# Two-layer hybrid encoder trunk: the mixer's vector work in the order of its inputs, without filler products, and its output projection begun over the tiles that are ready

## The reference, cut to what matters

```python
for l in range(DEPTH):                      # DEPTH = 2
    shift, scale, gate = ada_modulation(c, w_ada[l, 0], b_ada[l, 0])
    h = rmsnorm(x, g_norm[l, 0]) * (1.0 + scale) + shift
    y = hybrid_mixer(h, positions, l, ...)
    x = x + gate * rmsnorm(y, g_norm[l, 1])
    ...
    y = swiglu(h, ...) if l % 2 == 0 else moe_swiglu(h, ...)
    x = x + gate * rmsnorm(y, g_norm[l, 3])

def hybrid_mixer(h, ...):
    (q1, q2, k1, k2, va, qb, kb, vb, ob, ib, fb, cq, ckv, kr) = jnp.split(h @ w_in, split_idx, axis=-1)
    out_a = diff_attention_group(q1, q2, k1, k2, va, ...)       # 4 heads: 8 softmax units
    out_b = mlstm_group(qb, kb, vb, ob, ib, fb, ...)            # convolution, gates, 6 heads
    out_c = mla_group(cq, ckv, kr, ...)                         # 6 heads, rotary part
    return jnp.concatenate([out_a, out_b, out_c], axis=-1) @ w_out
```

## Time and profile before

| | |
|---|---|
| median of 3 runs | 1777.48 us (1775.68 to 1781.73) |
| profiled execution, its own time | 1780.08 us |
| its span | 1778.3 us |
| PE, DVE, ACT, POOL busy | 1535.9, 711.9, 545.2, 63.3 us |
| mean granted TensorE clock | 0.936 of full speed |
| mean DMA rate | 275 GB/s |

### The profile page before, as it was taken

The page is one execution under the profiler, slowest core; times in us unless marked ns, Lnnn a source line. Parts: engine busy times, 40 slices in busy tenths (PEclk is TensorE's granted clock), DMA queues, the critical chain, the costliest instruction groups (busy, mean ns, idle before and its releaser), DMA issues.

```text
span 1778.3 us, 30628 instructions
## 1 busy us (share of the span) xinstructions
PE 1535.9 (86%) x12500; PEld 1230.3 (69%) x12501; DVE 711.9 (40%) x1022; ACT 545.2 (31%) x749; POOL 63.3 (4%) x66
## 2 busy tenths in 40 slices
PE   5998879999999988776566999979998659999894
PEld 3757759999977577564344886559987448888552
DVE  2153245555531622410003884136764035666212
ACT  2123133333321231210003673035562024554101
POOL 0010000000000100100000000000000000000002
PEclk8989989999999899988777999999999889999898
DMA  9714556545433234659999999997677996555694
GB/s 362 272 42 178 215 196 265 211 180 189 176 138 142 67 152 184 260 233 425 423 424 425 426 397 387 425 425 300 256 277 280 424 422 264 238 236 224 269 424 161
DMA packets 74562, 488.92 MB, mean 275 GB/s; under 512 B 9792, under 2 KB 13920, under 8 KB 16544
## 3 DMA queue, kind: packets, MB, share of 16 engines
q1 hardware_dynamic: 72176, 479.94, 67.1%
q10 hardware_dynamic: 1648, 4.59, 0.7%
q0 software_dynamic: 576, 2.10, 0.4%
HBM read 482.66 MB, written 3.93 MB: 274 GB/s over the span
## 4 chain that ended last, share of the span: by engine, by line
PE 75%; DMA 10%; DVE 5%; issue 4%; ACT 3%; POOL 1%; SPq 1%; ACTq 1%; POOLq 0%; DVEq 0%
PE PG L1289 8%; PE PG L1399 5%; PE PG L1333 5%; DMA ring<-in_experts 4%; PE Y L909 4%; PE TRB L1333 4%; DMA arena<-in_experts 4%; PE Y L1301 4%; PE Y L1361 4%; PE Y L1173 3%; PE Y L917 3%; PE PG L873 3%; PE PG L874 3%; PE PG L875 3%; PE TRB L1339 3%
## 5 line engine op out<-in xcount | busy, mean ns | idle before, releaser
L1289 PE MATMUL PG<-ring,mixT 128*32 128x128 f32 (+1 forms) x1920 | 116.9, 347 | 61.2 <-issue 61.2
L1482 ACT ACTIVATE parts<-ring 128x2048 fp32r<-128x2048 f32 x84 | 158.5, 1906 | 12.3 <-PE Y L875 8.2
L1289 PEld LDWEIGHTS PG<-ring,mixT 128*32 128x32 f32 (+1 forms) x1920 | 89.5, 138 | 91.9 <-issue 76.7
L2272 DVE COPY arena<-TRB 128x64 f32<-128x64 f32 (+1 forms) x70 | 17.6, 252 | 335.6 <-PE TRB L1275 335.6
L1482 ACT ACTIVATE rope<-PG 64x128 f32<-64x128 f32 (+2 forms) x84 | 27.2, 324 | 373.0 <-PE PG L1289 348.4
L873 PE MATMUL PG<-h_parts,parts 128*128 128x256 f32 x448 | 127.5, 285 | 10.2 <-DVE parts L2148 10.2
L1289 PE MATMUL PG<-arena,mixT 128*32 128x128 f32 (+1 forms) x1664 | 98.9, 343 | 42.0 <-issue 42.0
L874 PE MATMUL PG<-h_parts,parts 128*128 128x256 f32 x448 | 127.3, 284 | 0.0
L875 PE MATMUL PG<-h_parts,parts 128*128 128x256 f32 x448 | 127.1, 284 | 0.0
L1289 PEld LDWEIGHTS PG<-arena,mixT 128*32 128x32 f32 (+1 forms) x1664 | 76.1, 135 | 69.5 <-issue 56.3
L2148 DVE TENSOR_TENSOR parts<-ring,parts 128x2048 fp32r<-128x2048 f32 x42 | 95.9, 2292 | 25.6 <-ACT parts L1482 25.4
(11 more groups left out here) (362 smaller groups left out, 2781.9 us busy)
## 6 DMA issues: line engine op xcount, KB each, us to landing
ring<-in_experts SPq DMA_DIRECT2D x168, 1024.0 KB, 13.3
arena<-in_experts SPq DMA_DIRECT2D x168, 1024.0 KB, 16.1
ring<-in_weights SPq DMA_DIRECT2D x116, 1024.0 KB, 6.1
ring<-in_weights SPq DMA_DIRECT2D x4, 512.0 KB, 4.3
ypairs<-hT ACTq DMA_DIRECT2D x3, 512.0 KB, 6.6
tok<-in_x SPq DMA_DIRECT2D x1, 1024.0 KB, 8.9
result<-scr SPq DMA_DIRECT2D x2, 512.0 KB, 2.6
ring<-in_weights SPq DMA_DIRECT2D x2, 432.0 KB, 6.3
```

Of the source, the lines that this page charges most:

```text
L1289: last = mm(bank[i * n:(i + 1) * n, 0:width], xe[:, k, 0:n], w[k // 4][:, k % 4, i * width:(i + 1) * width], start=(k == 0), stop=(k == KD ...
L1482: return nc.scalar.activation(out_, in_, func, **kw)
```

## The change

Five things are changed in both mixers.

1. The gate chain of the mLSTM goes to the head of the softmax work on ScalarE and VectorE. The convolution is cut in three parts of 8 operations, `conv(0)` to `conv(2)`, each behind its inputs, and `combine` follows its exponentials. The row maxima and exponentials of the last four A units go in TensorE's order (4, 6, 5, 7).
2. TensorE takes `at(0)` behind the second pair of A units and `at(1)` behind the last ones; `ada_rows` stands between the second and the third rotation. The three `busy` calls of the mixer are gone.
3. `pt(0)`, `c_unit(4)`, `pt(1)`, `c_unit(5)` stand between the two halves of the value projection `vb`; VectorE copies the halves out (`values`) in two places.
4. `bo` moves from the TR ring to the PJ ring.
5. The transposes into `mixT` are regrouped: `mt0` (tiles 0, 1) ahead of the mLSTM scores, `mt1` and `mt2` (5, 6, 7) behind `bo`, `mt3` and `mt4` (2, 3, 4) when `tok_ready` is set. Column blocks 2 and 3 of the output projection are computed over tiles 0, 1, 5, 6, 7 first and over 2, 3, 4 later; then blocks 0 and 1 follow. The third `ada_rows` stands between. The weight order is 2, 3, 0, 1.

```diff
-        uses.extend(("out", l, c) for c in range(D // SW))
+        uses.extend(("out", l, c) for c in OUT_ORDER)
...
+OUT_ORDER = (2, 3, 0, 1)
+MIX_EARLY, MIX_LATE = (0, 1, 5, 6, 7), (2, 3, 4)
...
                 def at(h):
                     bank = take_tr((f"at{h}", l))
-                    if h >= 2:
-                        busy(bank, 4 if h == 2 else 2)
...
                 def pt(u):
-                    if u == 1:
-                        busy(bank, 4)
...
+                at(0)
                 fm_pair("qk1", keys[6])
                 for b in range(TB):
                     a_units((2, b), (3, b))
+                at(1)
                 fm_pair("qk2", keys[7])
...
+                turn(0)
+                turn(1)
                 ada_rows(ADA_MIXER[l][1])
-                at(0)
-                at(1)
+                turn(2)
+                turn(3)
...
+                for b in range(TB):
+                    pe.wait_ge(*tr_done(f"co{b}", l))
+                turn_mixed("mt1", 5, 6)
+                turn_mixed("mt2", 7)
...
+                for i in range(3):
+                    pe.wait_ge(*tr_done(f"mt{i}", l))
+                for b in range(2):
+                    sc_over(b)
+                    mixed(2 + b, MIX_EARLY)
+                ada_rows(ADA_MIXER[l][3])
+                pe.wait_ge(tok_ready, l + 1)
+                turn_mixed("mt3", 2, 3)
+                turn_mixed("mt4", 4)
+                ada_columns(ADA_MIXER[l][3])
+                pe.wait_ge(*tr_done("mt3", l))
+                pe.wait_ge(*tr_done("mt4", l))
+                for b in range(2):
+                    mixed(2 + b, MIX_LATE).then_inc(out_read, 1)
+                for b in range(2):
+                    sc_over(2 + b)
+                    pe.wait_ge(pj_free[b], len(PJ_LAYER) // 2 * (l + 1))
+                    mixed(b, MIX_EARLY)
+                    mixed(b, MIX_LATE).then_inc(y_full if b else out_read, 1)
...
                 ada_rows(ADA_MIXER[l][0])
+                ae.wait_ge(gate_in, l + 1)
+                run(g_e[0:BH, :], g_n[0:BH, :], ACT.Exp).then_inc(gate_exp, 1)
...
+                negmaxes("a", 0, 1)
+                conv(0)
                 combine(0)
...
+                values(0)
                 r = root(("a", l))[:, 0:8].rearrange("p (b h o) -> p b h o", b=TB, o=1).to_broadcast([P, TB, AH, AV])
```

More of the change, by code:

```diff
@@ L1052, in mixer, with turn @@
                 pe.wait_ge(*pj_done("uq2", l))
-                for i in range(4):
+                def turn(i):
                     bank = take_sc((("rot", i), l))
@@ L1103, in mixer, with turn_mixed @@
                 last.then_inc(tr_full, 1)
+                def turn_mixed(name, *tiles):
+                    bank = take_tr((name, l))
+                    for j, f in enumerate(tiles):
+                        for b in range(TB):
+                            last = nc.tensor.transpose(bank[:, j * T + b * P:j * T + (b + 1) * P],
+                                                       tok[:, b, f * P:(f + 1) * P], ident)
+                    last.then_inc(tr_full, 1)
+                pe.wait_ge(*tr_done("ao", l))
+                turn_mixed("mt0", 0, 1)
                 pe.wait_ge(qks_ready, l + 1)
@@ L1141, in mixer @@
                 for b in range(TB):
[L1142 removed]
+                    bank = take_pj((f"bo{b}", l))
                     for h in range(BH):
@@ L1147, in mixer @@
                             last = mm(o, scw[:, h, c:c + P], vbx[:, kb, h, :], start=(kb == 0), stop=(kb == b))
[L1148 to L1169, removed]
+                    last.then_inc(pj_full, 1)
+                for b in range(TB):
+                    pe.wait_ge(*tr_done(f"co{b}", l))
@@ L1170, in mixer, with mixed @@
+                turn_mixed("mt1", 5, 6)
+                turn_mixed("mt2", 7)
+                def mixed(c, tiles):
                     s = slot("out", c)
                     for j in range(2):
-                        for k in range(KD):
+                        for k in tiles:
                             last = mm(Yk[:, 2 * c + j, :], ring[:, s, k, j * P:(j + 1) * P], mixT[:, k, :],
-                                      start=(k == 0), stop=(k == KD - 1))
-                    last.then_inc(out_read if c < D // SW - 1 else y_full, 1)
+                                      start=(j == 0 and k == 0), stop=(k == MIX_LATE[-1]), skip_group_check=True)
+                    return last
@@ new lines, in sc_over @@
+                def sc_over(b):
+                    pe.wait_ge(sc_free[b], len([i for i in range(len(SC_LAYER) * (l + 1)) if i % 4 == b]))
+                for i in range(3):
[7 more added lines that the diff above has]
+                turn_mixed("mt4", 4)
@@ L1613, in mixer @@
                 run(em[:, :], bank[:, 12:24], ACT.Exp).then_inc(free, 1)
+                bank, free = tr_item("mt0")
+                run(mixT[:, 0:2, :], bank.rearrange("p (a t) -> p a t", a=2), ACT.Copy, scale=gd[:, l:l + 1]).then_inc(free, 1)
                 ae.wait_ge(*tr_done("gt", l))
@@ L2079, in mixer @@
                 ve.wait_ge(obt_ready, l + 1)
-                bank, free = tr_item("mt1", l)
+                bank, free = tr_item("mt3", l)
                 for j in range(2):
@@ L2084, in mixer @@
                 last.then_inc(free, 1)
-                bank, free = tr_item("mt2", l)
-                V.scalar_tensor_tensor(mixT[:, 4, :], bank[:, 0:T], gml[:, l, 2:3], obt[:, 2, :], ALU.mult, ALU.mult)
-                V.tensor_copy(mixT[:, 5, :], bank[:, T:2 * T]).then_inc(free, 1)
+                bank, free = tr_item("mt4", l)
+                V.scalar_tensor_tensor(mixT[:, 4, :], bank[:, 0:T], gml[:, l, 2:3], obt[:, 2, :], ALU.mult,
+                                       ALU.mult).then_inc(free, 1)
                 ada(ADA_MIXER[l][3])
```

123 lines of the change are left out of this document (63 added, 60 removed).

## The result

The changed kernel takes 1750.18 us (median of 4 runs, 1746.31 to 1754.32), the kernel before 1777.61 in the same session: ratio 0.9844, 95% interval 0.9824 to 0.9864. It is 27 us faster, where 44 were forecast; 1750 lies above the range of 1728 to 1747. The profiled execution took 1752.9 us.

What follows compares the result with a forecast made beforehand. TensorE, nearly without pause in both mixers, was taken as the bound: its products, few waits and half-clock work. Gains of 20.7 us (mixer 0) and 23.2 (mixer 1), together 43.9, gave 1733.6 us, range 1728 to 1747.

Steps and rivals of the forecast that it cites:

- Gate chain first: Ahead of the rotations: gate chain moved before the first row maxima, ending near 84; the 2.35 us pause goes.
- Clock around the rotations: Rotations and conditioning product run at full clock without the pause ahead: gains of 2.96 and 2.32 us a mixer.
- the split: Rotations divided into 1.7 and 1.3 us, both shorter than the 2.35 us rest before the fall, so full clock.
- Rival B: Clock falls again at rotations and conditioning product (1744) or among transposes with short waits (1743); both 1753; chance 0.22.
- The Trainium skill's rule: Transposes don't count as clock work like products; stretches of `pt` and `mt` transposes would be rest, sum up to 9 us smaller.
- Filler of `at` and `pt(1)`: In each mixer, filler and waits at `at` go, gain 3.2 us; waits and filler at `pt(1)` go, net 7.0.
- The wait for VectorE at `pt(1)`: New wait: VectorE takes `values(0)` before the product freeing the bank of `pt(1)`; TensorE waits about 0.4 us.
- Output projection: From `bo` to the projection: early products hide group B's chain, waits of 4.4 become 1.5, gain 2.9 us a mixer.
- rivals D and E: Transfers give TensorE's gain back, no effect, chance 0.03; or late tiles of `vb` stall the engines, slower, chance 0.03.

Runs made afterwards that it cites:

- the padded kernel: The whole change plus 66 TensorE instructions at the start (16 one-column products and three met waits), experts' code where it was before: 1734.58 us.
- -42 and -26: The changed kernel with 24 more instructions (met waits) and with 40 more (10 one-column products) at TensorE's start: 1743.53 us and 1745.30 us.
- the first part alone: Against the changed kernel: output projection in the order of before, 74 padding instructions at the start; vector order, rotations and removed filler kept: 1741.81 us.
- the second part alone: Against the kernel before: only the output projection over the ready tiles first; vector order, filler and rotations of before: 1771.53 us.
- the last pair of runs: The whole change with 74 instructions of met waits ahead of `x`, 1733.03 us, and with 75 in three places where TensorE is idle, 1733.58 us.

## Why the prediction was wrong

**The step that failed:** "The dense part in between is TensorE's own work and the experts' transfers start on `y_full`, so both move as a whole." The dense part did (303.5 and 303.6). The experts grew by 15.3 us. The sum had no term for what fewer instructions do to code that is reached by branches. The 16.6 us between forecast and result are these 15.3 and 2.0 of the start, less 0.7 that the mixers gave above the forecast. At the position of before the same change takes 1734.6, against the forecast 1733.6; that they are so close is in part luck, since in its trace the padded kernel is 1.7 us shorter up to mixer 0 and 2.6 in the dense part than before, and 3.3 longer in the rest. That the position is the cause is shown from both sides, by the change without it and by it without the change, and the first run followed it product by product (26, 14, 6, whole). That a wait for the next block of instructions is how the position acts is the reading that fits these counts and the packets; no row shows the wait itself. The wide experts lose only at the change's position, the narrow ones also at -42 and -26; which single pause belongs to which landing was not resolved, nor why the pause ahead of the last expert is 9.5 to 9.9 at those two. Why the rest of the padded change is up to 5 us longer than that of others at its position stays open.

**Gate chain first.** Right: it runs from 82.73 to about 86.0 on VectorE, where about 84 was forecast for its end, still ahead of the first row maxima (88.07), and the 2.35 us are gone.

**Clock around the rotations.** The gain came (1.90 and 1.47 for the rotations, where 1.7 and 1.3 were forecast, and 3.66 for the product). The reason given for it, the split, was wrong: together they run at full clock too. What the runs leave of the reason is the missing pause, which the prediction also named; that the number held although the split does nothing is in part luck. Rival B did not occur at either of its places. The Trainium skill's rule (TensorE: Matmul & The Clock Gate, Part 4, PE-mode transpose) did not cost anything in this change: the clock was 1.00 through the stretches of transposes of 0.8 to 1.3 us with waits of up to 0.9 about them. Whether the rule is right, no run here shows: where the clock fell among transposes, in mixer 1 before and with the first part alone, a wait of 2.37 us stood ahead of them.

**Filler of `at` and `pt(1)`.** Right in size: mixer 0 as a whole gained 21.0 with 20.7 forecast, mixer 1 23.6 with 23.2, and from the end of the first half of `vb` to the second `ada_rows` it is 10.3 us (149.62 to 159.94), where 10.7 was forecast. With its filler back a mixer gave up 4.2. The wait for VectorE at `pt(1)` was put at 0.4 and is 0.47. The convolution, cut in three, costs VectorE 0.9 us more, put at 0.8.

**Output projection.** 2.9 forecast; on top of the first part it is worth 3.0 in mixer 0 and 3.8 in mixer 1, of which 0.9 is clock. Waits of 0.90 and 0.69 stand there, 1.5 was forecast. With the second part alone mixer 1 gained 4.4, its slow projection (2.3) among them.

**Transfers (rivals D and E).** Neither occurred: no DMA ends a pause of TensorE in the rows of the mixers after.

**The start.** +2.0 us in the profiled execution, not forecast. In that stage the clock varies from kernel to kernel, as the last pair of runs shows; the mark ahead of mixer 0 lay between 69.5 and 74.2 in the kernels with up to 75 instructions added.

## What to carry to other kernels

When a part of the kernel that the change does not touch gets slower, compare its pauses "<-issue" first, and where code is reached by branches, add a few harmless instructions ahead and see whether the pauses move: here 66 were worth 15.6 us, beside the 27 that the change showed. Where the instructions come from counts little: products, waits and the filler served alike. A comparison of two versions of such a kernel is fair only at the same position within the block of 256 instructions. Filler that holds the clock is to be tried again once the pause it covered is gone.

## What the runs showed of the hardware

- Code reached by a branch, moved by 24 to 66 instructions against blocks of 256: a run of products broken by 0.7 to 4.6 us (after 26, 14 or 6 of its 128 products), and 4.4 us ahead of the wide expert where there was no pause. Moved by a whole 256 (the control) the breaks are the same. The packet count follows: 118 in all runs at positions 0 to +9, 121 in the changed kernel, 120 and 121 at -42 and -26.
- An instruction that only waits for a semaphore already met takes about 0.1 us of TensorE's queue: 74 of them stand between the arrival of the constants, at 6.3 to 6.6 us by the runs padded with products, and the first transposes at 14.8. A product of one column with its weight load takes about 0.2 (94 in 20.2 us).
- TensorE's first transposes started 3.9 us later and it reached mixer 0 4.2 us sooner: the clock of the products behind was 1.00 instead of 0.50 in the stretch at 33 us. A rest of 1.58 us in mixer 0 was followed by a fall of the clock to 0.57, a rest of 1.52 at the same place in mixer 1 left the product behind at 3.66 us.
